# A two-layer block and a mixture-of-experts block on one core: lag-form state-space stage, other order of the even layer's first part, finer waits in the odd layer

## The reference, cut to what matters

```
hn = rmsnorm(x, even_norm)                      # even layer
q, k, v, u = split(hn @ even_w_in, [512, 640, 768])
q, k = rmsnorm(q, q_norm), rmsnorm(k, k_norm)   # per head of 64
o_attn = swa_sink_attention(q, k, v, sinks)
o_ssm  = s5_mixer(u, ...)
x = x + concat(o_attn, o_ssm) @ even_w_out

def s5_mixer(u, ...):                           # 32 groups of 16 channels, 64 complex states
    bb = w * b                                  # per group [64, 16], complex
    h[t] = lam * h[t-1] + bb @ u[t]
    y[t] = re(c @ h[t]) + d_skip * u[t]
    y = gelu(y)
    return y * sigmoid(y @ w_glu + b_glu)

q, k, v = split(rmsnorm(x, odd_norm) @ odd_w_in, 3)   # odd layer, 16 heads
x = x + stick_breaking_attention(q, k, v) @ odd_w_out
```

## Time and profile before

| | us |
|---|---|
| median of 3 runs (lowest, highest) | 1356.43 (1355.74, 1357.25) |
| the profiled execution: its own time | 1355.75 |
| its span | 1353.5 |
| PE busy | 1165.8 (86%) |
| DVE busy | 675.1 (50%) |
| ACT busy | 468.5 (35%) |
| POOL busy | 24.9 (2%) |

### The profile page before, as it was taken

The page is one execution under the profiler, slowest core; times in us unless marked ns, Lnnn a source line. Parts: engine busy times, 40 slices in busy tenths (PEclk is TensorE's granted clock), DMA queues, the critical chain, the costliest instruction groups (busy, mean ns, idle before and its releaser), DMA issues.

```text
span 1353.5 us, 19860 instructions
## 1 busy us (share of the span) xinstructions
PE 1165.8 (86%) x8152; PEld 920.2 (68%) x8152; DVE 675.1 (50%) x962; ACT 468.5 (35%) x599; POOL 24.9 (2%) x82
## 2 busy tenths in 40 slices
PE   6989999999999999999999999989566665657665
PEld 5887999998998999998998999973122121212211
DVE  7997565556688755556567877642011010101012
ACT  5456343334557443333453635431010010101001
POOL 2210000000000000000000000000000000000000
PEclk9889999999999999999999999989888787878879
DMA  9622365555444365555654545979999999999995
GB/s 247 141 58 93 125 218 187 186 186 186 154 157 125 125 217 186 184 186 171 214 156 125 186 156 181 414 312 422 422 421 422 422 422 422 422 422 422 422 421 208
DMA packets 137015, 343.40 MB, mean 254 GB/s; under 512 B 9818, under 2 KB 99036, under 8 KB 112372
## 3 DMA queue, kind: packets, MB, share of 16 engines
q1 hardware_dynamic: 135292, 337.96, 66.7%
q0 software_dynamic: 1552, 4.47, 1.8%
q10 hardware_dynamic: 104, 0.02, 0.0%
HBM read 339.80 MB, written 2.62 MB: 253 GB/s over the span
## 4 chain that ended last, share of the span: by engine, by line
PE 61%; DMA 23%; DVE 10%; issue 2%; ACT 2%; SPq 2%; POOL 0%; DVEq 0%; POOLq 0%; ACTq 0%
PE ps L1321 15%; PE ps L1323 15%; PE ps L1322 15%; DMA ring<-in_w_exp_down_dram 12%; DMA ring<-in_w_exp_up_dram 11%; PE ps L1840 4%; PE ps L1865 3%; DVE piece_lo L2040 1%; SPq L531 1%; PE ps L1188 1%; PE ps L1346 1%; PE ps L1339 1%; PE ps L1341 1%; PE ps L1461 1%; PE ps L1786 1%
## 5 line engine op out<-in xcount | busy, mean ns | idle before, releaser
L2040 DVE TENSOR_TENSOR piece_lo<-ring,piece_hi 128x2048 fp32r<-128x2048 f32 x118 | 266.9, 2285 | 66.6 <-ACT piece_hi L779 65.9
L1321 PE MATMUL ps<-HT_hi,piece_hi 128*128 128x256 f32 x1008 | 285.9, 284 | 0.0
L1323 PE MATMUL ps<-HT_hi,piece_lo 128*128 128x256 f32 x1008 | 285.1, 283 | 0.0
L1322 PE MATMUL ps<-HT_lo,piece_hi 128*128 128x256 f32 x1008 | 285.0, 283 | 0.0
L779 ACT ACTIVATE piece_hi<-ring 128x2048 fp32r<-128x2048 f32 x118 | 223.0, 1912 | 174.0 <-PE ps L1323 148.4
L1840 PE MATMUL ps<-ring,arena 128*32 128x512 f32 x992 | 142.4, 727 | 87.0 <-DMA ring<-in_w_exp_up_dram 66.8
L1321 PEld LDWEIGHTS ps<-HT_hi,piece_hi 128*128 128x128 f32 x1008 | 193.2, 192 | 2.0 <-issue 0.9
L1322 PEld LDWEIGHTS ps<-HT_lo,piece_hi 128*128 128x128 f32 x1008 | 193.2, 192 | 0.9
L1323 PEld LDWEIGHTS ps<-HT_hi,piece_lo 128*128 128x128 f32 x1008 | 193.2, 192 | 0.0
L1840 PEld LDWEIGHTS ps<-ring,arena 128*32 128x32 f32 x992 | 38.9, 130 | 184.3 <-issue 183.7
L1865 PE MATMUL ps<-ring,arena 128*32 128x512 f32 x464 | 76.2, 765 | 52.3 <-DMA ring<-in_w_exp_down_dram 52.3
(11 more groups left out here) (459 smaller groups left out, 1816.4 us busy)
## 6 DMA issues: line engine op xcount, KB each, us to landing
ring<-in_w_exp_gate_dram SPq DMA_DIRECT2D x64, 1024.0 KB, 18.6
ring<-in_w_exp_up_dram SPq DMA_DIRECT2D x60, 1024.0 KB, 17.8
ring<-in_w_exp_down_dram SPq DMA_DIRECT2D x58, 1024.0 KB, 16.2
ring<-in_ffn_w_gate_dram SPq DMA_DIRECT2D x22, 1024.0 KB, 5.8
ring<-in_ffn_w_up_dram SPq DMA_DIRECT2D x22, 1024.0 KB, 5.4
ring<-in_ffn_w_down_dram SPq DMA_DIRECT2D x22, 1024.0 KB, 7.4
ring<-in_w_in_dram SPq DMA_DIRECT2D x20, 1024.0 KB, 5.4
ring<-in_odd_w_in_dram SPq DMA_DIRECT2D x12, 1024.0 KB, 5.3
```

Of the source, the lines that this page charges most:

```text
L1321: pe.matmul(out, sh, mh, start=start, stop=False, skip_group_check=True)
L1322: pe.matmul(out, sh, ml, start=False, stop=False, skip_group_check=True)
L1323: return pe.matmul(out, sl, mh, start=False, stop=stop, skip_group_check=True)
L2040: ve.tensor_tensor(piece_lo[k % RING][:, :], ring[:, k % RING, :], piece_hi[:, h % HI_SLABS, :].bitcast(F32), ALU.subtract).then_inc(split, 1)
```

## The change

The diff is below, cut to its core. In words:

- `norm(0)` transposes the raw x. Its root is multiplied in later: for `u` by VectorE (`keep_u`, which also stores u by step), for `kv` and `q` by ScalarE (`empty_rooted`). The transposes come before the column tile, which now lies in bank 7 outside the plan. `ssm_c` is between the two pieces of `u`.
- The state-space weights are made dense on VectorE in one operation over 128 partitions, and ScalarE spreads them into block form with a mask as its scale (`spread_weights`). `ssm_c` is emptied by ScalarE. The chunk copies are made by ScalarE (steps 0, 1) and GpSimd (steps 2, 3).
- The products inside a chunk take lag form: for each of four lags, `lag_w` (a block-diagonal 128 x 128 matrix) times u shifted by the lag; `d_skip` is in lag 0. The outputs from the states are 64 products with 32 columns of weights per half. The output lies in PSUM by step with channels on partitions, so `outputs` and `skip` are gone and the GELU reads PSUM. `glu` and the gate work in step order. The 56 fillers are gone.
- `ssm_b_im` is loaded by SP's queue behind the two `u` pieces. The bias rows are stored once, and later repeated 127 times by a DMA from DRAM to DRAM.
- Odd layer: the scores of heads 0 to 3 wait only for the first tiles of q and k; the wait for `sb0_o` is gone; in half 1 `pt_even` is ahead of the third `odd_out` split; the third `ffn1` split is behind `norm_columns_split(3)`.

```diff
-TILE_PLAN = ([("cols", ["v"]), ("norm0", VA * 2), ("u", ["a"] * 2), ("ssm_c", ["v"] * 2), ("kv", ["a"]),
-              ("ssm_w", ["a"] * 8), ("q", ["a"]), ("ssm_k", ["a"]), ("q", ["a"]), ("swa_qT", ["a"] * 2), ("swa_kT", ["a"]),
+TILE_PLAN = ([("norm0", VA * 2), ("u", ["v"]), ("ssm_c", ["a"] * 2), ("u", ["v"]), ("kv", ["a"]), ("ssm_w", ["a"] * 8),
+              ("q", ["a"]), ("ssm_k", ["a"]), ("q", ["a"]), ("swa_qT", ["a"] * 2), ("swa_kT", ["a"]),
...
-GLU_FILLERS = 56
 FILLERS = {}
-RAW_NORMS = (1, 2, 3, 4)
+RAW_NORMS = (0, 1, 2, 3, 4)
...
+        state_half = ssm[:, 20, 0:2]
+        vtmp = [XN[:, i, :].rearrange("p (t j c) -> p t j c", j=CHUNK, c=GROUP_CH) for i in range(2)]
+        by_step = lambda v: v.rearrange("p (j i c) -> p j i c", j=CHUNK, i=2)
+        u_steps = [by_step(uT[:, 2 * half:2 * half + 2, :].rearrange("p i t -> p (i t)")) for half in range(2)]
+        in_order = lambda v: v.rearrange("p i (c j) -> p j i c", j=CHUNK)
...
+        def chunk_copy(half, r, j):
+
+            dst = U4[:, 8 * half:8 * half + 8, :].rearrange("p (i r) c -> p r i c", r=4)[32 * j:32 * j + 32, r]
+            return dst, u_steps[half][32 * r:32 * r + 32, j, :, :]
...
             group("u", w0, 768, 2)
+            sp.dma_start(braw[:, 1, :].rearrange("p (j c) -> p j c", c=GROUP_CH),
+                         a["ssm_b_im"][0].rearrange("(j g) n c -> (g n) j c", g=2)).then_inc(b_im_loaded, 16)
             group("kv", w0, 512, 1)
...
+            pool.memset(lag_w, 0.0)
...
-            for i, name in enumerate(("ssm_b_re", "ssm_b_im")):
-                pool.dma_start(braw[:, i, :].rearrange("p (j c) -> p j c", c=GROUP_CH),
-                               a[name][0].rearrange("(j g) n c -> (g n) j c", g=2)).then_inc(b_loaded, 16)
+            pool.dma_start(braw[:, 0, :].rearrange("p (j c) -> p j c", c=GROUP_CH),
+                           a["ssm_b_re"][0].rearrange("(j g) n c -> (g n) j c", g=2)).then_inc(b_loaded, 16)
             for i, name in enumerate(("ssm_c_re", "ssm_c_im")):
...
+            def chunked_inputs(half):
+                wait_emptied(pool, "u", half)
+                for r in range(4):
+                    for j in range(2, CHUNK):
+                        o.mark(pool.tensor_copy(*chunk_copy(half, r, j)))
+                pool.wait_ge(g_order, o.count)
+                pool.nop().then_inc(s_u4p, 1)
+
+            chunked_inputs(0)
             pool.wait_ge(s_decay, 1)
             pool.wait_ge(bank_full, full_count("ssm_c", 1))
...
+            chunked_inputs(1)
...
-            pool.dma_start(bias_dram, bias_row[:, :].unsqueeze(1).to_broadcast([8, P, 384])).then_inc(bias_stored, 16)
+            pool.dma_start(bias_dram[:, 0, :], bias_row[:, :]).then_inc(bias_stored, 16)
...
+            pool.dma_start(bias_dram[:, 1:P, :], bias_dram[:, 0:1, :].to_broadcast([8, P - 1, 384])).then_inc(bias_stored, 16)
+            pool.wait_ge(bias_stored, 32)
...
-            act.wait_ge(ident_ready, 1)
-            blank = ident[:, :].unsqueeze(1).to_broadcast([P, STATE_TILES, P])
-            for w in W2:
-                o.mark(act.activation(w[:, :, 1:, :].rearrange("p t d c -> p t (d c)"), blank, ACT.Copy, scale=0.0))
-            act.wait_ge(a_order, o.count)
-            act.nop().then_inc(s_wz, 1)
-            o.mark(act.activation(W3, blank, ACT.Copy, scale=0.0))
+            act.wait_ge(cols_ready, 1)
+            norm_columns(0)
             act.wait_ge(s_th, 1)
             act.activation(ssm[:, 9, :], ssm[:, 3, :], ACT.Exp, scale=float(CHUNK))
             act.activation(ssm[:, 4, :], ssm[:, 3, :], ACT.Exp).then_inc(s_decay, 1)
             act.activation(ssm[:, 7, :], ssm[:, 5, :], ACT.Sin)
             act.activation(ssm[:, 8, :], ssm[:, 6, :], ACT.Sin).then_inc(s_trig, 1)
...
+            act.wait_ge(consts_ready, 1)
+            act.wait_ge(ident_ready, 1)
+            for i in range(4):
+                act.activation(lag_w[:, i, 0, :], ident[:, :], ACT.Copy, scale=cols[:, ROW_D + i:ROW_D + i + 1])
+
...
+            def spread_weights(no, part, out, ready):
+                act.wait_ge(s_dense, no)
+                for g in range(2):
+                    o.mark(act.activation(out[:, :, :, 16 * g:16 * g + 16], (wtmp if part else vtmp)[0], ACT.Copy,
+                                          scale=state_half[:, g:g + 1]))
+                act.wait_ge(a_order, o.count)
+                act.nop().then_inc(ready, 1)
+
+            def empty_rooted(name, i, c0):
+                b = full_tile(act, name, i)
+                act.wait_ge(normed, 2)
+                for tb in range(2):
+                    ins = act.activation(qkv[:, tb, c0:c0 + 256], b[:, tb * 256:tb * 256 + 256], ACT.Copy,
+                                         scale=ms[:, 18 + tb:19 + tb])
+                ins.then_inc(emptied["a"], 1)
+
             act.wait_ge(ssm_loaded, 32)
...
+            chunked_inputs(0)
+            for i, sign in enumerate((1.0, -1.0)):
+                b = full_tile(act, "ssm_c", i).rearrange("p (t c) -> p t c", c=32)
+                act.activation(W2[i][:, :, 0, :], b, ACT.Copy, scale=sign).then_inc(emptied["a"], 1)
+            for part in range(2):
+                spread_weights(part + 1, part, W1n[part], s_w1)
+            chunked_inputs(1)
+            empty_rooted("kv", 0, 512)
+            input_weights(range(8))
             act.wait_ge(s_ph, 1)
...
+            spread_weights(3, 0, W2[0][:, :, 1:, :], s_w2)
+            spread_weights(4, 1, W2[1][:, :, 1:, :], s_w2)
+            empty_rooted("q", 0, 0)
...
-                for j in range(CHUNK):
-                    o.mark(act.activation(W3.rearrange("p (i r) c -> p r i c", r=4)[32 * j:32 * j + 32, r, :, 32 * j:P],
-                                          b[32 * r:32 * r + 32, :, 0:P - 32 * j], ACT.Copy))
+                own = slice(32 * r, 32 * r + 32)
+                o.mark(act.activation(lag_w[own, :, :, own], b[own], ACT.Copy))
             act.wait_ge(a_order, o.count)
...
+            def square(half):
...
+                act.activation(square_of(half).rearrange("p a b -> p (a b)"), ps[:, 4 + half, :], ACT.Square,
...
+            norm(0, wait=False)
             pe.wait_ge(rows_loaded, 16 * ROW_LOADS)
-            pe.transpose(open_tile(pe, "cols", 0)[:, 0:ROWS], rows[:, :], ident[0:ROWS, 0:ROWS])
+            pe.transpose(ps[:, 7, 0:ROWS], rows[:, :], ident[0:ROWS, 0:ROWS])
             pe.wait_ge(s_dt, 1)
-            pe.transpose(bank("cols", 0)[:, P:P + 16], dt_rows, ident[0:16, 0:16]).then_inc(bank_full, 1)
-            norm(0)
-            feature_major("u", 2)
+            pe.transpose(ps[:, 7, P:P + 16], dt_rows, ident[0:16, 0:16]).then_inc(cols_full, 1)
+            spread_roots(0)
+            wait_all_emptied(pe, "norm0")
...
+            token_major("kv", 1)
+            input_weights(range(8))
+            for half in range(2):
+                wait_emptied(pe, "ssm_w", 5 + 2 * half)
+                pe.wait_ge(s_u4, half + 1)
+                pe.wait_ge(s_u4p, half + 1)
+                chunk_inputs(half)
...
+            for t in range(STATE_TILES):
+                r, i = t % 4, t // 4
+                own = slice(32 * r, 32 * r + 32)
+                ins = pe.matmul(b[own, i * P:i * P + 32], lag_w[:, i, 0, own], ident[:, own], start=False, stop=True,
+                                skip_group_check=True)
...
-                for t in range(8 * half, 8 * half + 8):
-                    o = ps[:, 4 + half, CHUNKS * (t % 8):CHUNKS * (t % 8 + 1)]
-                    ins = pe.matmul(o, W3[:, t, :], U4[:, t, :], start=True, stop=False, skip_group_check=True)
-                    if t == 0:
-                        pay_piece(ins)
-                    for i in range(2):
-                        ins = pe.matmul(o[:, 1:CHUNKS], W2[i][:, t, 1:, :].rearrange("p d c -> p (d c)"),
-                                        Xs[i][:, t, 0:CHUNKS - 1], start=False, stop=(i == 1), skip_group_check=True)
...
+                y = by_step(ps[:, 4 + half, :])
+                for i in range(2):
+                    for d in range(CHUNK):
+                        ins = pe.matmul(y[:, d:, i, :], lag_w[:, 2 * half + i, d, :], u_steps[half][:, 0:CHUNK - d, i, :],
+                                        start=(i == d == 0), stop=False, skip_group_check=True)
+                        if i == d == 0:
...
+                for i in range(2):
+                    for j in range(CHUNK):
+                        for part in range(2):
+                            for r in range(4):
+                                t = 4 * (2 * half + i) + r
+                                ins = pe.matmul(y[32 * r:32 * r + 32, j, i, 1:CHUNKS], W2[part][:, t, j + 1, :],
+                                                Xs[part][:, t, 0:CHUNKS - 1], start=False, stop=(part == 1),
+                                                skip_group_check=True)
                 ins.then_inc(s_y, 1)
...
-            for _ in range(GLU_FILLERS):
```

(39 more changed lines are left out.)

243 lines of the change are left out of this document (97 added, 146 removed).

## The result

The changed kernel takes **1336.97 us**, the median of 4 runs (1336.44 to 1338.78), beside 1356.11 for the kernel before (1355.74 to 1357.25, 4 runs). The ratio is 0.9861, 95% interval 0.985 to 0.9873: 18.8 us less. Run again unedited later (c_changed_again), it was at 0.9857 (0.9842 to 0.9872).

The account below looks back on a forecast made before the run. TensorE was taken to bound the middle and the experts' weights the tail, which moves with the path before it. First part 6.3 plus odd layer 2.6 gave 8.9 us less: 1347.2 us, own range 1342 to 1351, wider range 1339.5 to 1353.5.

Parts of the forecast that it names:

- TensorE's order sets the pace: First part, to the outputs: VectorE's and ScalarE's shorter work leaves the path, so TensorE's order sets when outputs end, 81.0.
- Start, C, `u`, `kv`: Kernel start through input weights: `u` at about 12.0, 5.1 earlier, `ssm_c` done at 21.8, first `q` piece at 48.4.
- First `q` piece: Behind `chunk_inputs`: takes 9.46 us, the lower-clock duration, because the same 64-column work is ahead; at 7.07, 2.4 less.
- `ssm_k`: Between the two `q` pieces: 2.02 us for 64 records plus 32 records for `d_skip`, 3.0 us, to 60.9.
- The outputs: Lag-form output stage after the second `q`: both halves 13.0 us, 2.1 more than before, states' products 4.0 a half.
- From there to the scores: After the outputs: q and k transposes at 81.0, 5.7 earlier; ScalarE's work costs 1.0, so scores start 4.7 earlier.
- Scores to the projection: Masks, softmax and normalisation before the output projection: 15.4 us instead of 18.0, a further 2.6 earlier.
- The gate's clock: `glu` without fillers: at the lower level throughout, 5 us come out beyond the cover; 1 us of these charged.
- Odd layer: Three TensorE gaps at scores and `turn_probs` shortened: together 2.6 us saved, bounds 1 and 3.5.
- The bias store: GpSimd's bias store split, first part: nobody waits for it, so 0 us, bounds 0 and 2.
- Rival 1: TensorE quicker: `q` at 7.07, states' products at lower bound, no `glu` clock loss, odd layer 1 more: 1342; chance 0.17.
- Rivals 2 to 5: C late, 1353.7, chance 0.12; no overlap of states' products, 1357.7, 0.07; low clock stays, 1379, 0.04; tail cancels gain, 0.02.

Follow-up runs that it names:

- e3: Changed kernel with `ssm_b_im` issued by GpSimd again, ahead of the two C loads: ratio 0.9934 to the kernel before.
- e6: Changed kernel with the two column transposes moved ahead of x's sixteen, as before: ratio 0.9873 to the kernel before.
- e10: Changed kernel with GpSimd's 16 chunk copies given to VectorE: ratio 0.9888 to the kernel before.
- e14: Changed kernel with roots shared between VectorE and GpSimd, ScalarE's second tanh behind emptying the transposes, and 14 filler transposes in the third block: 1334.46 us, ratio 0.9836.
- e7: Changed kernel with one more TensorE wait, between the halves of `chunk_inputs`, for ScalarE's first output weights: ratio 0.9888 to the kernel before.
- b2: Kernel before with one edit alone, `ssm_b_im` issued by SyncE behind the `u` pieces: ratio 0.9977.
- b4: Kernel before with one edit alone, the bias row stored once and repeated within DRAM: ratio 0.9997.
- e5: Changed kernel with the states' products ordered column group outermost, 16 neighbours in one group: ratio 0.9933 to the kernel before.
- e12: Changed kernel with filler transposes in three idle times: 14 in the third block, 14 ahead of q and k's transposes, 17 ahead of the gate's product: ratio 0.9856.
- e1: Changed kernel with the four edits of the odd layer undone: ratio 0.9881 to the kernel before.
- e2: Changed kernel with the 56 filler transposes put back ahead of the gate's product: ratio 0.9857 to the kernel before.
- e11: Changed kernel with 14 filler transposes where TensorE waits for VectorE in the third block: ratio 0.9849 to the kernel before.
- e8: Changed kernel with bias rows stored 128 times from SBUF by one transfer, no repeat within DRAM: ratio 0.9915 to the kernel before.

## Why the prediction was right in direction and short in size

What failed is the price of the states' products in the lag-form outputs (4.0 us a half taken, 1.97 measured) and, with it, the path: "neither is on the path any more: TensorE is", where VectorE with GpSimd came last. The first `q` piece's 9.46 and four smaller terms erred the same way. By its own steps:

- **TensorE's order sets the pace**: right to 43.8 us (e3, e6), though VectorE is as late there to within 0.44 us (e10), and not from there on. VectorE with GpSimd is last until the transposes of q and k; that is read from the trace (dense from 43.80, TensorE's wait of 1.97), and from e14, where a shorter part of GpSimd brought them 0.5 earlier.
- **Start, C, `u`, `kv`**: 48.4 forecast for the first `q` piece, 47.08 measured: 1.3 us. C was not waited for, since it was issued at 10.64.
- **First `q` piece**: 9.46 taken, 7.13 measured: 2.3 us. I took the narrow work ahead of it for the cause of the low clock. The same work without a gap left the clock full, and a gap in it brought 9.52 back (e7). But with the 0.79 us of before the 9.46 was itself chance: b2 and b4 had 7.12 and 7.13 behind it. One profile was too few for this term.
- **`ssm_k`**: 3.0 taken, 2.2 measured: 0.8. The 32 records for `d_skip` took 0.53.
- **The outputs**: 13.0 taken, 8.86 measured, 4.1 us, the largest error. The lag products were right (2.5 a half). For the states' products I took L1531's 0.032 a record and overlooked that it has 128 moving columns and not 63; even my lower bound of 3.6 us a half was above the 1.97 measured, because it was a quarter of an untiled record's 0.114, and 0.114 is what 128 columns cost too. Fewer moving columns than 128 didn't help with weights of 128 columns; with weights of 32 they did: 0.052 alone in a group (e5). The Trainium skill's rule in "TensorEngine Tiling (Array Packing)", section Instruction Overhead, is some 60 cycles a matmul, an estimated 0.025 us. Taken for a record, as I took it, it doesn't hold: a record takes 0.0154. Taken for a product, of 0.031 us, it does.
- **From there to the scores**: 4.8 forecast, 4.9 measured, by luck: it holds a wait of 1.97 for GpSimd that I had excluded, and transposes at the full clock for the low one.
- **Scores to the projection**: 20.3 forecast, 19.2 measured: 1.1. No run takes this step apart; before it took 22.9, with the scores at the low clock.
- **The gate's clock**: 1.0 taken off; the clock did fall (8.83 for 7.07), but the product stayed hidden beside the softmax (e12): 1.0.
- **Odd layer**: 2.6 forecast, 3.0 measured by the leads, 3.1 by e1.
- **The bias store**: "0 (bounds 0 and 2 us)". As an edit of the kernel before that is right (b4). In the new kernel it is worth 7.6 us. I asked who waits for the transfer, and not what it does to the new stage beside it. It is no part of the error, as the changed kernel has the split.

The terms add up: 1.3 + 2.3 + 0.8 + 4.1 + 1.1 + 1.0 = 10.6 beyond the 6.3 of the first part, measured 17.2; with 0.4 more in the odd layer and 1.5 taken by the third block's clock that is 18.4 for 18.8. In the first part all err to the same side, so no error hid another. Rival 1 had the right sign for three of them, but took its price for the products from the same bound, and the clock that it left full at the gate did fall. Rivals 2 to 5 didn't occur; the 1.5 in the third block lies ahead of the experts and is chance. Of what I named as proof, the second `q` ended at 63.4 instead of 68, and the transposes came at 74.2 and not 81, released by GpSimd.

## What to carry to other kernels

Before a row stands in for an operation that the trace doesn't have, compare all of its sizes: I matched the 32 columns of weights and missed the 63 moving ones. Ask of a low clock which gap is ahead of it, not which work, and take a second profile before its price goes into a sum. Ask of an edit that looks idle what it protects in the new stage, since removing it there and adding it alone to the old kernel gave 7.6 us and 0. When leads are compared over a long program, take them at several milestones, so that a stretch that varies by itself isn't booked to an edit.

## What the runs showed of the hardware

- The same 1.8 to 2.0 us of idle TensorE, behind the same instructions, left the granted clock at 1.00 in some executions (changed kernel twice) and at 0.50 in others (e2 and e11, 76 to 80 us), which came to 0.7 us at the scores and, in e11, 1.8 at the projection. In the third block it came out as 0, 1.5 or 3.0 us, and the 0.79 us gap of the kernel before as 7.1 or 9.3 to 9.5 for the piece behind it.
- A transfer of 1.5 MB out of 8 partitions takes 34 us to land; the repeat within DRAM takes 12.1. Beside the first, the 16 KB transfers of the instruction queue came 11 us (e8) and 13 us (before, by b4) later, and in e8 a run of short TensorE instructions stood for 5.2 us.
- Two `ssm_b` loads behind each other on GpSimd's queue cost 6.85 us of idle time; `ssm_b` and the two C loads cost none.
- Eight 32x128 copies: 8.1 us on GpSimd beside a busy VectorE, 3.6 beside a mostly idle one (e3), 2.0 to 2.7 on VectorE. A 128x640 multiplication on VectorE beside one on GpSimd took 1.93 us; another 128x640 operation, on VectorE alone, had taken 0.78.
